# Mixture-of-experts start of a fused decoder layer: two kept weight loads wait for the first token gather, and the shared expert's down product runs behind the first pair's up product

## The reference, cut to what matters

```python
h2 = rmsnorm(x, lw['g_norm_ffn']) * (1.0 + scale_f) + shift_f       # 264 tokens x 1024
gates = sigmoid_topk_gates(hb, lw['w_router'], lw['b_router'])      # top 8 of 64 experts
a = jnp.einsum('td,edf->tef', hb, lw['w_e_gate'])                   # 64 x (1024 x 256)
b = jnp.einsum('td,edf->tef', hb, lw['w_e_up'])                     # 64 x (1024 x 256)
routed = jnp.einsum('tef,efd->td', jax.nn.silu(a) * b * gates[..., None], lw['w_e_down'])
shared = (jax.nn.silu(hb @ lw['w_sh_gate']) * (hb @ lw['w_sh_up'])) @ lw['w_sh_down']
return routed + shared
```

## Time and profile before

| | |
|---|---|
| median of 3 runs | 997.11 us (995.99 to 997.92) |
| profiled execution, first to last instruction (span) | 996.5 us |
| PE busy in it | 970.8 us (97%) |
| DVE busy | 610.7 us (61%) |
| ScalarE busy | 187.9 us (19%) |
| POOL busy | 56.7 us (6%) |
| HBM read | 315.80 MB |

### The profile page before, as it was taken

The page is one execution under the profiler, slowest core; times in us unless marked ns, Lnnn a source line. Parts: engine busy times, 40 slices in busy tenths (PEclk is TensorE's granted clock), DMA queues, the critical chain, the costliest instruction groups (busy, mean ns, idle before and its releaser), DMA issues.

```text
span 996.5 us, 14013 instructions
## 1 busy us (share of the span) xinstructions
PE 970.8 (97%) x4542; PEld 547.3 (55%) x4542; DVE 610.7 (61%) x1563; ACT 187.9 (19%) x385; POOL 56.7 (6%) x81
## 2 busy tenths in 40 slices
PE   6999999999999999999989999999999999999997
PEld 2487766444547778888743444444444444444443
DVE  3603322468754011133738898898898898888875
ACT  3311231345444100002510100000000000001000
POOL 0100010100000000000210000000000000000000
PEclk9999999999999999999989999999999999999999
DMA  8994469555555583554679999999999999999991
GB/s 310 420 413 195 177 240 325 174 162 167 164 156 215 203 331 132 211 189 159 232 290 420 424 421 427 424 420 424 427 421 425 425 422 403 421 422 423 427 413 65
DMA packets 55211, 311.88 MB, mean 313 GB/s; under 512 B 8954, under 2 KB 28442, under 8 KB 33266
## 3 DMA queue, kind: packets, MB, share of 16 engines
q1 hardware_dynamic: 48834, 297.21, 75.2%
q0 software_dynamic: 6320, 13.93, 3.9%
HBM read 315.80 MB, written 3.95 MB: 321 GB/s over the span
## 4 chain that ended last, share of the span: by engine, by line
PE 82%; DMA 7%; SPq 5%; DVE 3%; issue 2%; ACT 0%; DVEq 0%; POOLq 0%; ACTq 0%
PE bank L789 48%; PE pA L789 21%; PE pB L789 6%; PE pC L789 5%; DMA ring<-in_w_e_gu 5%; SPq L456 3%; SPq L500 1%; SPq L495 1%; DMA xs<-h_rows,idx 1%; DMA pT<-in_poolT 1%; PE bank L1341 1%; PE pA L822 0%; PE pD L789 0%; DVE xT L2355 0%; DMA ring<-in_poolT 0%
## 5 line engine op out<-in xcount | busy, mean ns | idle before, releaser
L789 PE MATMUL pA<-ring,qT 128*64 128x512 f32 x976 | 228.5, 597 | 2.6 <-DMA ring<-in_w_e_gu 2.5
L2343 DVE STREAM_TRANSPOSE qT<-xs 32x256 f32<-32x256 f32 x480 | 209.2, 436 | 7.7
L789 PE MATMUL bank<-hT,ring 128*128 128x264 f32 (+1 forms) x832 | 189.3, 388 | 2.3 <-ACTq L1616 2.3
L789 PEld LDWEIGHTS bank<-hT,ring 128*128 128x128 f32 (+1 forms) x832 | 154.3, 189 | 35.6 <-issue 10.0
L789 PEld LDWEIGHTS pA<-ring,qT 128*64 128x64 f32 x976 | 72.1, 137 | 130.7 <-issue 126.8
L789 PE MATMUL bank<-pT,vtok 128*128 128x264 f32 x512 | 127.9, 393 | 0.3 <-DVE pT L2435 0.3
L789 PEld LDWEIGHTS bank<-pT,vtok 128*128 128x128 f32 x512 | 92.0, 190 | 39.3 <-issue 26.7
L2352 DVE TENSOR_TENSOR pT<-pT,bank 128x264 f32<-128x264 f32 x248 | 99.9, 427 | 8.8 <-PE bank L789 7.3
L789 PE MATMUL bank<-wuk,ring 128*128 128x512 f32 x192 | 86.3, 597 | 0.0
L789 PE MATMUL pB<-ring,oaT 128*64 128x512 f32 x240 | 62.0, 605 | 0.0
L789 PE MATMUL pC<-ring,oaT 128*64 128x512 f32 x240 | 60.3, 592 | 0.0
(11 more groups left out here) (344 smaller groups left out, 813.9 us busy)
## 6 DMA issues: line engine op xcount, KB each, us to landing
ring<-in_w_e_gu SPq DMA_DIRECT2D x61, 2048.0 KB, 17.3
ring<-in_w_e_dn SPq DMA_DIRECT2D x60, 1024.0 KB, 16.2
ring<-in_poolT SPq DMA_DIRECT2D x64, 208.0 KB, 2.8
ring<-in_w_ada SPq DMA_DIRECT2D x12, 1024.0 KB, 10.4
ring<-in_w_bg SPq DMA_DIRECT2D x4, 3072.0 KB, 11.5
ring<-in_w_mix SPq DMA_DIRECT2D x5, 2048.0 KB, 14.9
ring<-in_w_ada SPq DMA_DIRECT2D x4, 2048.0 KB, 13.9
ring<-in_poolR SPq DMA_DIRECT2D x56, 128.0 KB, 2.3
```

The costliest lines, as they stand in the source:

```text
L789: return nc.tensor.matmul(out, lhsT, rhs, start=start, stop=stop)
L2343: last = V.transpose(xTs[32 * j:32 * j + 32, q % 2, :, 32 * a:32 * a + 32], src[32 * a:32 * a + 32, j])
```

## The change

- SP waits for the first gather (`d_x[0]` at 16) before step 2 above, so steps 2 to 4 lie behind this wait.
- Step 5 (wait for the end of the shared down product, down weights of expert 4) moves into `first_up`, so behind the up weights of expert 5 and ahead of the 2 MiB of expert 43.
- On PE all 8 parts of `shared_down` move from around `slots(1)` to behind `up(0)` and ahead of `tokens_tr(1)`.
- On DVE the 8 `shared_sum` copies, and the wait for their banks, move into pair 0 behind the gated activation. `index(0)`, `index(1)` and `pick_experts(2)` now follow each other.
- The bank numbers follow: the uses of `slots` 0, 1 and 2 stand together ahead of the shared expert's.

```diff
-          ("shgu1", 1), ("shup1", 1), ("posT", 1), ("gt0", 1), ("shdn0", 4), ("gt1", 1), ("shdn4", 4),
-          ("moe", 10 * (E // 2) - 2), ("fgates", 4), ("fexp", 12 * E)]
+          ("shgu1", 1), ("shup1", 1), ("posT", 1), ("gt0", 1), ("gt1", 1), ("gt2", 1), ("shdn0", 4), ("shdn4", 4),
+          ("moe", 10 * (E // 2) - 3), ("fgates", 4), ("fexp", 12 * E)]
-USE["G", 0], USE["G", 1] = BASE["gt0"], BASE["gt1"]
+USE["G", 0], USE["G", 1], USE["G", 2] = BASE["gt0"], BASE["gt1"], BASE["gt2"]
 for _p in range(NPAIR):
-    if _p + 2 < NPAIR:
+    if _p and _p + 2 < NPAIR:
         _use("G", _p + 2)
...
             sp.wait_ge(full[n % 4], n // 4 + 1)
+            sp.wait_ge(d_x[0], 16)
             sp.dma_start(hTf[:, 0:1024], A["w_e_gu"][KEPT][:, 6:8].rearrange("p k c -> p (k c)")).then_inc(d_kept, 16)
...
             sp.dma_start(part(2, 0, DT, 2 * FE), A["w_e_gu"][4]).then_inc(wgt[2], 16)
-            reuse(2, "exp")
-            sp.dma_start(part(2, 2 * DT * FE, FT, D), A["w_e_dn"][4]).then_inc(wgd[2], 16)
 
             def first_up():
+                reuse(2, "exp")
+                sp.dma_start(part(2, 2 * DT * FE, FT, D), A["w_e_dn"][4]).then_inc(wgd[2], 16)
                 sp.dma_start(adx[:], A["w_e_gu"][AGAIN][:, 0:CT]).then_inc(d_first, 16)
...
                 up(p, i)
                 if p == 0:
+                    pe.wait_ge(s["act"], 2)
+                    shared_down(range(8))
                     tokens_tr(1)
...
             slots(0, None)
-            pe.wait_ge(s["act"], 2)
-            shared_down(range(0, 4))
             slots(1, None)
-            shared_down(range(4, 8))
             tokens_tr(0)
...
+                if p == 0:
+                    shared_sum(range(8))
+                    for b in range(4):
+                        n = BASE["shdn4"] + b
+                        dve.wait_ge(free[n % 4], n // 4 + 1)
                 if p:
                     add(p - 1, i, range(8))
...
             index(0, None)
-            shared_sum(range(0, 4))
             index(1, None)
             pick_experts(2, None)
-            shared_sum(range(4, 8))
-            for b in range(4):
-                n = BASE["shdn4"] + b
-                dve.wait_ge(free[n % 4], n // 4 + 1)
             gate_column(0, None)
```

## The result

The median is 999.61 us, beside 997.11 us for the kernel before (11 runs of each): ratio 1.0025, 95% interval 1.0014 to 1.0037. One of the 11 executions of the kernel after was in a slow state (3578.91 us) and does not enter the ratio; the median of the other ten is 999.52 us. So the change makes the kernel slower, by about a quarter of a per cent; the interval has the 0.2% at which the prediction draws its line inside it. Measured again later, with before run beside it, the ratio was 1.0015 (1.0005 to 1.0024), 999.20 us beside 997.25. The forecast of 998.6 us was 1.0 us too low for the first measurement; its +1.5 us is about what the second shows (+1.95 by the medians, +1.5 by the ratio). The profiled execution took 997.72 us, the lowest of the 11; its span is 996.0 us, *less* than the 996.5 us of before.

The account below looks back on a forecast made before the run. PE was taken to set the expert stage's end, with the DMA queue near its limit and causing 2.5 us of waits. PE's path +3.9 and stalls -2.4 gave +1.5 us: 998.6 us (+0.15%), range 996.6 to 1001.5.

Parts of the forecast that it names:

- Part 1, the gather: First gather, with the loads held back: lands 4.2 us after issue, at 504.65 instead of 508.6, -4.0 us on PE's path.
- Part 2, the shared product: Shared down product behind the first up product: nothing covers it, +7.7 us on PE, plus 0.2 us for two hand-overs.
- Part 3, the clock: PE's clock after the wait for the first gather: low in both kernels, so 0 us taken for the first up product.
- The bounds: Limits on the clock's effect on the first up product: 1.8 us gained if back before it, 5.2 us lost if low throughout.
- The path's sum: PE's path to pair 1's up product: -4.0 + 7.7 + 0.2 = +3.9 us, start at 530.1 instead of 526.2.
- Parts 4 and 5, the queue and the stalls: SP's weight queue 2.5 us better off against PE; the later 2.5 us of waits for up weights shrink, -2.4 us.
- The lead is lost: Rival, slower: the queue runs empty after 537 us, the stall at 957 stays; +2.9 us, 1000.0, or +3.9, 1001.0; chance 0.25.
- The gather is hardly faster: Rival, slower: the first gather lands after 6.2 us, +3.5 us in all, 1000.6; at 8.2 us, +5.5; chance 0.12.
- Faster: Rival: gather lands after 2.9 us and PE's clock is back before the up product; -1.6 us, 995.5; chance 0.13.
- within 0.2%: Outcome class for the whole kernel: same time, to within about 0.2% (2.0 us); given 0.51, against slower 0.42 and faster 0.07.

Follow-up runs that it names:

- after_again: The kernel after, unaltered, profiled and measured again on one chip with the warmed kernels: 999.20 us, beside 997.25 us for before.
- the first profile: The profiled execution of the unaltered kernel before on which the prediction rests: span 996.5 us, mean granted clock 0.996.
- before_look1: The kernel before, unaltered, profiled a second time: 996.03 us.
- before_look2: The kernel before, unaltered, profiled a third time: 996.31 us.
- the warmed kernels: Idle matmuls added in PE's wait for the first gather: 30 in the kernel after, 997.70 us (1.0000); 13 in the kernel before, 996.64 us (0.9987).
- hold_only: The kernel before with only the new SP wait for the first gather's landing; shared product and expert 4's down weights unmoved: 996.27 us, ratio 0.9983.
- hold_to_issue: As hold_only, but SP waits only until the first gather is about to be issued (turn at 1): 1003.31 us, ratio 1.0048.
- move_only: The kernel after without the new SP wait; shared product, its sums and expert 4's down weights still moved: 1007.79 us, ratio 1.0099.

## Why the prediction was right, and where it was not

Every sign that the prediction names for being right came: landing after 4.2 us, PE's wait of 7.2 us, `up(0)` in 8.7 and 9.1 us, the shared product of 7.3 us behind it, pair 1's up product at 528.8 and 531.2 us, and no waits for up weights.

**Part 1, the gather: right.** Predicted 4.2 us, measured 4.23 and 4.22, from the one row whose surroundings were alike. The estimate of 3.3 us, from the Trainium skill's page "DMA: Bandwidth & Descriptors", section "Anatomy of one DMA", was 0.9 us too low for this transfer: no first gather here landed in under 4.2 us (a second one, issued while the first is moving, took 4.0 us in the kernel after and 3.6 in after_again). Beside the first profile the gain is the 4.0 us predicted; beside before_look1 and before_look2 (7.08 and 7.80) it is 3.2 us. The number is right, but the prediction has the gather share the engines with the loads ahead of it. The packets (last section) show that in before it mostly stood behind them, 4.1 to 4.3 us of its 7.1 to 8.2.

**Part 2, the shared product: right.** It costs its full 7.32 us on the path (7.7 predicted). The hand-overs gained 0.2 us instead of costing it: from its end to pair 1's up product it is 5.89 us (522.88 to 528.77), where it was 6.07 from the end of `up(0)` before (520.14 to 526.21): the four transposes took 0.45 us instead of 0.60. One reading of the rows is wrong: the 7.7 us did not all stand in the gather's 8.2 us. The product began at 497.74, 2.7 us before the gather's issue, so 5.1 us of it (500.45 to 505.55) stood there and the rest in front, where PE would have waited for the indices. The sum does not hang on it, since all of it was covered.

**Part 3, the clock: a value from one row, not settled.** "I take 0" holds beside the first profile (8.71 and 9.12 us beside 8.82, and 2.70 us from landing to `up(0)` in both). Beside before_look1 and before_look2 it does not: there `up(0)` takes 7.9 us and landing to `up(0)` 2.26 us, so the kernel after loses +1.4 us on the path. Over all executions the mean granted clock is 0.992 to 0.995 for the kernel after and mostly 0.996 for before, so it is low for longer after the change. How much of that falls on work and not on waiting the mean does not say, and the warmed kernels do not tell 0 from 1 us. The bounds (1.8 gained, 5.2 lost) hold either value; the argument for 0, one row and the same work behind it, does not choose between them.

**The path's sum.** Predicted +3.9. Measured (the mean of the two profiles of after, 29.05) +3.3 against the first profile (25.8) and +5.4 against the other two (23.7). The parts of the latter: -3.2 landing, +7.3 shared product, +1.4 clock, -0.2 hand-overs, 5.3 in all.

**Parts 4 and 5, the queue and the stalls: right.** Predicted a lead of 2.5 us and -2.4 us of stalls; measured landings 4.1 to 4.4 us shorter, which is more than the lead predicted, waits of 2.5 us (2.8 and 2.9 in the other two profiles) down to 0, and 2.9 us less from up(1) to the end beside the first profile (470.3 less 467.4), 3.3 beside the other two (470.7 less 467.4). With the path's +3.3 and +5.4 this makes +0.4 and +2.1 us. The medians say +1.95 and +2.5.

**The rivals.** "The lead is lost" is refuted: no wait for up weights is left. The DMA share at 845 to 846 us, on whose dip it rested, is 0.73 in the kernel after and 1.12 in after_again, so the dip in that window comes and goes by execution. "The gather is hardly faster" is refuted by 4.2 us. "Faster" needed the clock back before the up product; it was not. The rule "Issue the DMA early, do compute, wait on its semaphore late" (the Trainium skill, page "DMA: Bandwidth & Descriptors", section "Rules for kernel authors") is what the pair hold_only and after tests: the same wait on SP, with the shared product in front of PE's wait or behind it. In front it gives 0.9983, behind it 1.0025 and 1.0015. The trace agrees with the rule, and the price of leaving it here is 3 to 4 us (3.3 by the table's sums, 496.5 less 493.2).

**The class.** The likeliest case was "within 0.2%", at 1.5 us. The first measurement (2.5 us, 0.14 to 0.37%) is past the line and the second (0.05 to 0.24%) is short of it, so the runs do not decide the class. That the forecast lies this near is in part luck: two profiles more of the kernel before would have moved its base by up to 2 us, as much as the whole effect.

**Left open:** what the clock costs the kernel before when no idle matmul overruns the landing, and so whether part 3 is 0 or +1.4 us.

## What to carry to other kernels

Bulk loads that nobody needs yet can be worth holding back until a small transfer on the critical path has *landed* (0.9983 here); holding them only until its issue can be worse than nothing (1.0048). Keep compute in front of that wait: moved behind it, the product cost its full 7.3 us, and the idle engine's clock fell as well. And before a sum is built on differences of 1 us, read the same stretch in several executions, and check with the times and clocks of unprofiled ones which profile is typical: three profiles of one kernel differed here by 2.1 us, as much as the effect, and the typical execution lay between them.

## What the runs showed of the hardware

**The first gather starts about when the loads issued ahead of it are through, and then shares.** The packets of POOL's queue (q0), looked up in windows of half a microsecond, show when the first gather's bytes begin to move. SP's queue (q1) had these bytes issued ahead of the gather, and had moved these by then:

| kernel | SP bytes issued ahead | moved when the gather starts | start after issue | landing |
|---|---|---|---|---|
| after, hold_only | 1.57 MB | 1.57, 1.57 MB | 1.6, 1.4 us | 4.2, 4.4 us |
| before, before_look1, before_look2 | 3.15 MB | 2.84, 2.91, 2.94 MB | 4.1, 4.2, 4.3 us | 8.2, 7.1, 7.8 us |
| hold_to_issue | 2.62 MB | 2.68 MB | 5.1 us | 12.6 us |
| move_only | 3.15 MB | 3.02 MB | 5.0 us | 12.2 us |

The same as lines of the queue view (packets, MB, share of 16 engines), from SP's first load to the gather's first window: hold_only, 496 to 502.5 us, and hold_to_issue, 494.8 to 505 us.
```profile
q1 hardware_dynamic: 144, 1.57, 71.8%
```
```profile
q1 hardware_dynamic: 469, 2.68, 80.5%
```
With nothing left ahead, the start is still 1.4 to 1.6 us after the issue. In the other rows it came late by about the time that the bytes ahead still needed. DVE's work is not what delays it: in move_only DVE is idle from 502 to 512 us and the start takes 5.0 us; in hold_only DVE is busy 2.8 of the 4 us from 500 to 504 and the start takes 1.4 us.

The share that the gather then got differs. The queues of before from 505 to 507 us, and of move_only from 508 to 510 us:
```profile
q1 hardware_dynamic: 107, 0.44, 67.7%
q0 software_dynamic: 129, 0.27, 39.9%
```
```profile
q1 hardware_dynamic: 43, 0.70, 82.1%
q0 software_dynamic: 43, 0.14, 17.1%
```
In move_only SP's 2 MiB, issued 0.2 us behind the gather, took 82% and left it 17%. But the distance of that load is not the whole cause: in hold_to_issue it is 2.84 us, as in before (2.85), and the gather lands as late as in move_only. The Trainium skill, page "DMA: Bandwidth & Descriptors", section "Queues, rings and completion order", says that each engine takes turns between the queues that have work, a packet at a time. For the stretch in which both move, move_only agrees: equal packets (43 and 43), but 16 KB to 3 KB of bytes each (0.70 and 0.14 MB over 43), so equal turns are not equal shares. For the start it does not: by turns the gather would have begun some 1.5 us after its issue, as in hold_only, beside the loads ahead. What orders it behind them is not settled by these runs.
